# Second mixer of a two-layer encoder on one core: its products placed between the chunks of its input projection, and the output tiles of its differential half in one block at the end

## The reference, cut to what matters

```
hn = rms_norm(h)
cq, ckv, kidx, widx, dq, dk, dv = split(hn @ od_w_in)      # 16 tiles of 128 columns
o_c = dsa_mixer(...)                                       # 8 heads of 64
#   index score = sum over 4 index heads of relu(q_idx . k_idx) * w; keep the 128 best keys of each
#   query; softmax over these alone
o_d = rms_norm((softmax(s1) - lam * softmax(s2)) @ v) * (1 - lam_init)   # 4 heads, two softmaxes each
h = h + concat(o_c, o_d) @ od_w_out
```

## Time and profile before

| | |
|---|---|
| median of three executions | 2103.39 us |
| the profiled execution's own time | 2105.17 us |
| span of the profiled execution | 2103.3 us |
| share of the span: TensorE / its weight loads / VectorE / ScalarE / GpSimd | 96% / 77% / 49% / 30% / 15% |
| DMA moved | 179.60 MB |

### The profile page before, as it was taken

How to read it: one execution, slowest core, us unless ns; L and a number is a source line. 1 busy time by engine, 2 the same in 40 slices (tenths; PEclk the granted TensorE clock), 3 DMA queues, 4 the chain that set the end, 5 groups by cost and what they waited for, 6 DMA issues and landing times.

```text
span 2103.3 us, 24455 instructions
## 1 busy us (share of the span) xinstructions
PE 2016.4 (96%) x8908; PEld 1612.0 (77%) x8908; DVE 1036.6 (49%) x1638; ACT 634.5 (30%) x938; POOL 306.6 (15%) x280
## 2 busy tenths in 40 slices
PE   7999999888999999999999999998699999999997
PEld 5888888666788888887888888885455888888886
DVE  5444426861554443346544433455974454443345
ACT  4232222222433222223323222224424333232222
POOL 2000001621400000124000001300334400000124
PEclk9999999885999999999999999999858999999998
DMA  4323232220232323322323232331000222223321
GB/s 159 102 91 99 90 110 80 85 67 21 80 100 90 100 89 110 110 80 90 100 80 110 90 110 91 107 100 41 1 1 7 94 100 93 99 87 110 110 81 50
DMA packets 56732, 179.60 MB, mean 85 GB/s; under 512 B 12145, under 2 KB 12145, under 8 KB 56657
## 3 DMA queue, kind: packets, MB, share of 16 engines
q1 hardware_dynamic: 48032, 171.00, 24.7%
q10 hardware_dynamic: 7712, 4.79, 0.9%
q0 software_dynamic: 928, 3.02, 0.5%
HBM read 175.04 MB, written 3.15 MB: 85 GB/s over the span
## 4 chain that ended last, share of the span: by engine, by line
PE 86%; DVE 8%; POOL 2%; issue 2%; ACT 1%; ACTq 0%; DMA 0%; POOLq 0%; DVEq 0%
PE ps L1516 53%; PE ps L1528 24%; PE ps L1818 2%; PE ps L1854 1%; PE ps L1612 1%; DVE w_lo L309 1%; PE ps L1831 1%; DVE sm L879 1%; DVE work L854 1%; DVE m_b L542 1%; POOL sm L1111 1%; POOL sumsq L1038 1%; DVE stat L852 0%; DVE rstd L343 0%; PE ps L1734 0%
## 5 line engine op out<-in xcount | busy, mean ns | idle before, releaser
L1516 PE MATMUL ps<-x_hi,w_hi 128*128 128x512 f32 x1728 | 683.6, 396 | 28.5 <-DVE x_lo L337 13.1
L1516 PE MATMUL ps<-x_lo,w_hi 128*128 128x512 f32 x1728 | 677.8, 392 | 0.0
L1516 PE MATMUL ps<-x_hi,w_lo 128*128 128x512 f32 x1728 | 677.5, 392 | 0.0
L309 DVE TENSOR_TENSOR w_lo<-raw,w_hi 128x1024 fp32r<-128x1024 f32 x322 | 410.1, 1288 | 473.8 <-ACT w_hi L301 468.1
L301 ACT ACTIVATE w_hi<-raw 128x1024 fp32r<-128x1024 f32 x322 | 332.5, 1050 | 378.1 <-PE ps L1528 314.5
L1516 PEld LDWEIGHTS ps<-x_hi,w_hi 128*128 128x128 f32 x1728 | 327.7, 190 | 104.3 <-issue 18.0
L1516 PEld LDWEIGHTS ps<-x_lo,w_hi 128*128 128x128 f32 x1728 | 328.0, 190 | 69.6 <-issue 2.2
L1516 PEld LDWEIGHTS ps<-x_hi,w_lo 128*128 128x128 f32 x1728 | 327.6, 190 | 68.9
L1528 PE MATMUL ps<-act_hi,w_hi 128*128 (+1 forms) x816 | 319.3, 391 | 2.8 <-DVE act_lo L710 1.4
L1528 PE MATMUL ps<-act_lo,w_hi 128*128 (+1 forms) x816 | 318.4, 390 | 0.0
L1528 PE MATMUL ps<-act_hi,w_lo 128*128 (+1 forms) x816 | 318.4, 390 | 0.0
(11 more groups left out here) (341 smaller groups left out, 1384.3 us busy)
## 6 DMA issues: line engine op xcount, KB each, us to landing
raw<-in_weights SPq DMA_DIRECT2D x322, 512.0 KB, 3.3
h<-in_xT ACTq DMA_DIRECT2D x4, 512.0 KB, 6.9
out<-result SPq DMA_DIRECT2D x4, 512.0 KB, 3.0
p_raw<-in_pT POOLq DMA_DIRECT2D x2, 512.0 KB, 4.0
scratch_u<-u_sc ACTq DMA_DIRECT2D x1, 512.0 KB, 2.8
u_grp<-scratch_u ACTq DMA_DIRECT2D x1, 512.0 KB, 4.2
scratch_y<-y_grp ACTq DMA_DIRECT2D x2, 256.0 KB, 3.3
y_ch<-scratch_y ACTq DMA_DIRECT2D x1, 512.0 KB, 3.5
```

The lines of the kernel that those rows point to most:

```text
L309: dve.tensor_tensor(w_lo[:, slot], raw[:, slot], w_hi[:, slot].bitcast(F32), SUB)\
L1516: last = pe.matmul(ps[:, bank], w[:, slot, k], x[:, k], start=(k == 0 and part == 0), stop=(k == KD - 1 and part == 2))
```

## The change

It rewrites the four parts of the second mixer (od_pe, od_dve, od_act, od_pool), places its tiles in memory anew, and changes the order of some weight chunks. It does this:

- The order of the input chunks is now cq, cq, ckv, kidx/widx, and then dq, dk, dv of head 0, of head 1, of head 2, of head 3 (OD_IN_ORDER). From the fifth chunk on their results go alternately into banks 0 and 1.
- Index queries come after chunk 3, index scores after chunks 4, 5 and 6, the transposes of the dv of a head after chunks 7, 10 and 13 (the last in group 12).
- There are 32 units in 35 groups, which are stages of one pipeline: group k has the scores of unit k, the transposes of unit k - 2 and the values of unit k - 3. Units 0 to 15 are d, a head at a time. Units 16 to 31 are c, with two heads each, in blocks m = 0 to 3. Groups 0 to 11 stand in the slots of chunks 7 to 15 (slot_of_group: 7, 7, 8, 9, 10, 10, 11, 12, 13, 13, 14, 15).
- All 48 rounds of the choice are in VectorE's slots 5 to 15: one behind each mask of a group, the others (SELECTS) at the end of a slot. The normalization of the latents moves to slot 13.
- q, k and v of c are made in groups 12 to 17 (c_prep, 16 products of 512 columns).
- The maximum and its bias are one instruction. GpSimd's scalings are gone. d is mixed unnormalized, and its sums and its norm come in at the end; c is scaled once for each block, after its values. Values come out with the queries on partitions, and are transposed afterwards (16 transposes for d, 16 for c).
- The sums of squares of d are ScalarE's (accumulated on four Square instructions for each head), so TensorE's sums and spread products are gone (L1871, L1881).
- The gains of the latents are multiplied into the small weights by GpSimd (w_gained, six instructions).
- The output projection is tile by tile. All eight tiles of the d rows come first (LAST_TILES), each added into h by VectorE (add_part). Then the last c block is transposed, and the eight tiles of the c rows follow. Both have the same matmuls as before, 192 in all.

```diff
+SELECTS = {5: 2, 6: 3, 7: 3, 8: 4, 9: 4, 10: 4, 11: 4, 12: 4, 13: 3, 14: 4, 15: 4}
...
+        def od_dve(dve):
...
+            def mask(u):
...
+                for s in (2 * u, 2 * u + 1):
+                    dve.wait_ge(od_s["scores"], s + 1)
+                    dve.tensor_tensor_reduce(
+                        out=sm[s % len(sm)][:, 0:keys], in0=ps[:, 2 + s % 2, 0:keys], in1=added,
+                        scale=-SCALE, scalar=-LOWEST, op0=ADD, op1=ALU.min,
+                        accum_out=job[:, 0, s:s + 1]).then_inc(od_s["masked"], 1)
...
+            for j in range(OD_IN):
+                scale(j)
+                split_lo(dve, first, AHEAD + 2 + j)
...
+                if j in (5, 6, 7):
+                    dve.wait_ge(od_s["const"], 2)
+                    combine(j - 5)
+                for k in groups_of_slot(j):
+                    mask(k)
+                    select(1)
+                    mix(k - 1)
+                if j == 13:
+                    latents()
+                select(SELECTS.get(j, 0))
+            for k in range(Z_GROUPS, GROUPS):
+                if k < UNITS:
+                    mask(k)
+                mix(k - 1)
+                select(1)
...
+        def od_act(act):
...
+            def d_out(u):
+                if not 0 <= u < D_UNITS or u % NQ != NQ - 1:
+                    return
+                hh = u // NQ
+                act.wait_ge(od_s["pv"], u + 1)
+                act.activation(o_d[:, hh], ps[:, 7], ACT.Copy).then_inc(od_s["d_raw"], 1)
+                for m in range(NQ):
+                    cols = slice(m * P, (m + 1) * P)
+                    act.activation(unused[:, hh, cols], ps[:, 7, cols], ACT.Square,
+                                   accum_out=stat[:, 4, NQ * hh + m:NQ * hh + m + 1])\
+                       .then_inc(od_s["d_raw"], 1)
...
+        def od_pe(pe):
...
+            def scores(u):
...
+                for n in range(2):
+                    s = 2 * u + n
+                    if u:
+                        pe.wait_ge(od_s["masked"], s - 1)
+                    else:
+                        pe.wait_ge(od_s["std"], n + 1)
+                    rows = slice(HD * n, HD * n + HD)
+                    if kind == "d":
+                        lhs, rhs = dq[rows, a % 2, queries], dk[rows, a % 2, 0:keys]
+                    else:
+                        lhs, rhs = q_t[rows, b, queries], k_t[rows, b, 0:keys]
+                    pe.matmul(ps[:, 2 + s % 2, 0:keys], lhs, rhs, start=True, stop=True)\
+                      .then_inc(od_s["scores"], 1)
...
+            def group(k):
+                if k < UNITS:
+                    scores(k)
+                turn(k - 2)
+                values(k - 3)
...
+            for j in range(OD_IN):
+                if j >= 4:
+                    pe.wait_ge(z_ready, zb + (j - 3 if j < 6 else j - 1))
+                in_chunk(pe, first, j, od_bank(j), n=5 if j == 0 else None)
...
+                for k in groups_of_slot(j):
+                    group(k)
+            for k in range(Z_GROUPS, GROUPS):
+                group(k)
+                if k == Z_GROUPS:
+                    values_in(3)
+                if 2 * (k - Z_GROUPS) < len(C_PREP):
+                    c_prep(2 * (k - Z_GROUPS))
+                    c_prep(2 * (k - Z_GROUPS) + 1)
...
+            for t in LAST_TILES:
+                d_tile(t)
+            c_turn(NQ - 1)
+            pe.wait_ge(od_s["c_lo"], NQ)
+            for group_ in range(2):
+                place = STARTS[7] + 4 + 2 * group_
+                pe.wait_ge(split_ready, place + 2)
+                if group_:
+                    pe.wait_ge(od_s["part_added"], KD)
+                for d in range(GROUP):
+                    out_tile(place, 0, d, (4, 0)[group_] + d, tile_done)
```

More of the change, by code:

```diff
@@ L195, in encoder @@
[L195 to L202, removed]
+        cq = over("cq", [P, 2, T], free_hi)
@@ L785, in od_in_dve @@
                 else:
[L786 to L817, removed]
+                    hh, kind = divmod(j - 4, 3)
@@ L823, in od_dve @@
                     dve.scalar_tensor_tensor(
[L824 to L832, removed]
+                        out=kept[b][:], in0=relu[:, i, 0:keys], scalar=weight,
+                        in1=kept[b][:] if i else causal[:, T - keys:], op0=MULT, op1=ADD)\
@@ L834, in do @@
+                       .then_inc(od_s["index_step"], 1)
+            chosen = [0, 0]
             def do(ins):
@@ new lines, in mask @@
+            def mask(u):
+                kind, a, b = unit_of(u)
+                keys = keys_of(u)
+                m = keys // QB - 1
+                if kind == "c" and m in CHOOSING:
+                    select(ROUNDS * (CHOOSING.index(m) + 1) - chosen[1])
+                added = kept[CHOOSING.index(m)][:] if kind == "c" and m in CHOOSING \
+                    else causal[:, T - keys:]
+                if u >= 3:
+                    dve.wait_ge(od_s["turned"], turns_before(u - 2))
+                for s in (2 * u, 2 * u + 1):
[4 more added lines that the diff above has]
+                        accum_out=job[:, 0, s:s + 1]).then_inc(od_s["masked"], 1)
@@ L1796, in od_pe @@
                                      start=True, stop=True)
-                elif kind == "v":
+                else:
                     last = pe.matmul(ps[:, bank], ckv[:, i * QB:(i + 1) * QB], w_uv[:],
                                      start=True, stop=True)
-                else:
-                    for head in range(4):
-                        last = pe.transpose(ps[:, bank, head * P:(head + 1) * P],
-                                            dv[:, head, i * QB:(i + 1) * QB], ident[:])
@@ L1804, in od_pe @@
-                last.then_inc(od_s["prep"], 1)
-            def scores(u):
-                kind, m, hh = UNITS[u]
-                queries, keys = slice(m * QB, (m + 1) * QB), (m + 1) * QB
-                for n, s in enumerate(JOBS_OF[u]):
-                    if s >= 3:
-                        pe.wait_ge(od_s["masked"], s - 2)
-                    half = n if kind == "d" else hh % 2
-                    rows = slice(HD * half, HD * half + HD)
-                    if kind == "d":
-                        lhs, rhs = dq[rows, hh, queries], dk[rows, hh, 0:keys]
-                    else:
-                        lhs, rhs = q_t[rows, hh // 2, queries], k_t[rows, hh // 2, 0:keys]
-                    pe.matmul(ps[:, s % 3, 0:keys], lhs, rhs, start=True, stop=True)\
-                      .then_inc(od_s["scores"], 1)
```

848 lines of the change are left out of this document (532 added, 316 removed).

## The result

The changed kernel takes 2070.35 us (median of 4 runs, 2068.98 to 2072.03), the kernel before 2104.54 beside it: ratio 0.9842, 95% interval 0.9824 to 0.986. That is 33 us faster. The forecast was 2079, range 2060 to 2118. The profiled execution took 2068.98 us, span 2067.2.

A forecast was written before the change was run, and what follows sets the result against it. VectorE binds the chunks from slot 7, then TensorE works from 1521 to 1597; the mixer ends at 1643.4 against 1670.1. 26.7 less 2.5 for the clock gives 24.2 us gain: 2079 us, range 2060 to 2118.

The forecast's parts named there:

- VectorE's slots: Input-chunk slots 5 to 15: VectorE binds from slot 7; slots 7 to 15 add 113.5 us, last selection ends at 1518.
- The clock beside the chunks: Slots 7 to 15: TensorE idles four or five times for 3 to 8 us, then restarts at half rate; 2.5 us lost.
- TensorE's remainder: Groups from 1521 at full clock: 70.3 us of TensorE work, 76 with waits, ending at 1597.
- The 5.7 us for waits and the rest: Added to TensorE's 70.3 us: 2.5 for the last d head, 3.2 for lower clock, ScalarE and semaphores.
- The wait for the last head of d: First values of the last d head wait for five ScalarE instructions of the head before: 2.5 us.
- The table switches: Root of d: two ScalarE table loads of 1.28 us, 2.6 us hidden; at the skill's price 5.3, some 1.5 showing.
- ScalarE's pace: Smallest c units: part of 3.2 us added together with the rest of the lower clock and semaphores.
- Output: Output projection: d and c tiles 21.9 us each, 2.6 us between them for the last c block.
- Why so little of the hidden selection is gained: Input chunks: selection kept TensorE waiting until 1534 before; much is given back because chunks now wait for VectorE.
- The rival of the clock: Groups 12 to 34: the clock stays down in the c part, 45 us more, 2124 us; chance 0.18.
- the 8 us pause: At group 12: TensorE idle some 8 us waiting for VectorE's mask, so the lower clock is taken until 1521.

The follow-up runs named there:

- e6: The kernel before with 45 of its 48 selection rounds left out: 2108.19 us, ratio 1.0014.
- e5: The changed kernel with 45 of its 48 selection rounds left out: 2041.55 us, ratio 0.9711.
- e7: The changed kernel with 16 idle maxima on VectorE ahead of the mask of group 18, so TensorE pauses: 2081.87 us, ratio 0.9899.
- e12: The changed kernel with 16 idle VectorE maxima ahead of group 18's mask and each c unit's two score products apart: 2132.05 us, ratio 1.0138.
- e8: The changed kernel with each c unit's second score product issued behind the transposes, not directly behind the first: 2081.72 us, ratio 0.9901.

## Why the prediction was right, and where it was not

The time was 9 us under the forecast and well in the range. The place where the new kernel is bound, and the order in which its queues meet, came out as forecast. By its own steps:

- **VectorE's slots: right.** The closing round of 512 keys began at 1512.69, 167.7 us into the mixer; forecast 1514, which is 164.9, and 167.4 with the 2.5 for the clock. VectorE was busy 19.0 to 19.6 of each 20 us but one. Of five waits of TensorE for a mask the longest was 6.7 us (forecast: four or five of 3 to 8).
- **The clock beside the chunks: right as far as what follows tells.** It was 0.50 in five stretches, 51.3 us together, in which TensorE was busy for only 27.0. The remainder of TensorE's work (from the scores of unit 13, at 1518.93) began 173.9 us into the mixer; forecast 174.4. The term of 2.5 by itself wasn't measured.
- **TensorE's remainder: mis-sized, 76 us where it took 69.1** (1518.93 to 1588.05). This is the forecast's one error of weight. The 5.7 us for waits and the rest were right: TensorE was idle for 5.2. Its work was 70.3 in the sum and 64.0 in the trace, and the largest part of that is the price of the c values. I kept the old 0.255 us a product, against a lower bound of 0.148. Measured: 16 instructions in 1.73 us, 0.216 a product, 3.1 us less on 80. Transposes had 0.148 throughout; four still took 0.59 to 0.63, but eight took 0.87 to 1.02, about 1.5 less in all. Pairs of scores had the durations of their rows, and the next instruction began a little sooner (0.85 and 1.06 us on the chain, where I had 0.92 and 1.13): about 1 less. Preparation took 0.86 a product, not 0.91: 0.6 less. A c unit of 512 keys cost TensorE some 3.7 us, not 4.4.
- **The wait for the last head of d: right**, 2.1 us where I had 2.5.
- **The table switches: right by the trace's price.** ScalarE's timeline of the changed kernel:

```profile
1548.99 1.28 ACT L1613 ACT_TABLE_LOAD   x1
1550.28 0.22 ACT L1613 ACTIVATE stat<-stat 128x16 f32<-128x16 f32 x1
...
1551.06 1.28 ACT L1519 ACT_TABLE_LOAD   x1
1552.36 0.51 ACT L1519 ACTIVATE sm<-sm,job 128x256 f32<-128x256 f32 x1
```

  Each load is followed by its operation after 1.29 to 1.30 us, so there is no second part to the price. They did not hide altogether: ScalarE is on the chain here, and TensorE waited 2.3 us in three times for its copies. I had that under "ScalarE's pace".
- **Output: right**, 1.85 us between the halves, transposes included; forecast 2.6.
- **Why so little of the hidden selection is gained: wrong.** The prediction said that the selection kept TensorE waiting until 1534 before, and that its move beside the chunks was given back because VectorE became the bound there. e6 shows that the old kernel paid next to nothing for the selection as long as GpSimd's scalings stood beside it, and e5 that the new one pays 28 us. The sum didn't rest on it: I followed the new queues from their durations, and only the story around it fell. Had I costed the change as "what before waits for, less what is hidden", I would have been wrong.
- **The rival of the clock: wrong in its condition, and its price not tested like for like.** It said that either state keeps itself, and that the dense preparation products behind the 8 us pause speak against it. At that pause it was so: the clock rose among those products. But a pause at group 18, where none of them is left, cost 12 us (e7), not 45, and the clock came back with its paired scores. With single scores it did stay down, and e12's c part from group 18 to the d tiles took 94.8 us (1555.44 to 1650.28). I had priced a slow c part at 90, but for all sixteen units and with pairs; that the two numbers lie close is chance.

**Where the 32 us come from.** Half of TensorE's busy time at 0.50 is the clock's cost. This is an estimate: at 0.50 two transposes took 0.62 us and four value instructions 1.05, at 1.00 four took 0.59 and eight 1.02. Before it was busy 14.8 us in the first such stretch and 64.7 in the second, 79.5 / 2 = 39.8; after, 27.0 / 2 = 13.5; so 26.3 less. The busy time fell by 44.7 in all, so 18.4 are left for the work itself. Of these some 12 are the scores side by side, as far as e8 shows it; narrower values and the removed norm products less the added transposes must make up the others, which no run took one by one. Against this stand 12.6 us more of idle time, TensorE waiting for VectorE above all. 26.3 + 18.4 - 12.6 = 32.1; it comes out since the 18.4 is a remainder. The clock's term is the one that the change doesn't speak of at all. That the clock would stay up in the c part was forecast, against a rival at 0.18, and by the place where it rose, for the reason given; that this is the largest term of the gain I hadn't seen.

## What to carry to other kernels

A busy engine that another one waits for is not yet the only bound: ask what it would wait for if its work were gone, and leave the work out of both kernels to see. Forecast a reordering by following the new queues with measured durations, not by subtracting waits of the old profile. After any pause of TensorE look at the granted clock of what follows, and in what form the work stands there; products on half of the rows are worth pairing, here for 12 us of their own, and behind a pause for up to 50 more (e12 against e8, the pause included).

## What the runs showed of the hardware

- The same attention work behind a pause of TensorE ran at 0.50 for 92.1 us (pause 12.3), or came back after 23.9 (pause 8.0); the first had its score products single, the second in pairs. The Trainium skill ("TensorE: Matmul & The Clock Gate", section "What's actually happening") says that activity releases the throttle. The trace agrees for the changed kernel, at 1517.4 us, and in e7; in e12 the clock stayed down through 88.26 us of busy time.
- Splitting the pairs cost 12 us on 16 units, where durations foretold 9: two products of 512 keys take 1.06 to 1.11 us together and 1.05 each when apart.
- A VectorE operation with two inputs took up to 2.67 us in place of 0.63 beside a GpSimd operation, while MAX8 and MATCH_REPLACE8 were not slowed.
